# Weight sums of a block product made by accumulating DMAs from GpSimd in place of VectorE additions

## Chip, cores and metric

The kernel runs on one core of a Trainium2 chip. The metric is the device time of one execution in microseconds (us). The engines are named as in the profile: PE (TensorE matmuls), PEld (its weight loads), DVE (VectorE), ACT (ScalarE), POOL (GpSimd) and SP (SyncE, which issues most DMAs). SPq and POOLq are the DMA queues of SP and POOL.

## The reference, cut to what matters

The model is a two-layer decoder trunk on 256 tokens of width 2048 in float32. Layer 0 is an 8-head retention mixer, layer 1 a pooling mixer. The change touches heads 1 to 7 of layer 0 alone.

```python
def retention_branch(xn, w_in, w_out):              # 8 heads, dk 256, dv 512, chunk 128
    q, k, v, g = jnp.split(xn @ w_in, ...)          # w_in: 2048 x 12288
    q = rotate_pairs(q, cos, sin)
    k = rotate_pairs(k, cos, sin) * (dk ** -0.5)
    # scores = (q k^T) * decay, y = scores v (and the state between chunks)
    y = (y - mean(y)) * rsqrt(var(y) + GN_EPS)      # per head
    return (jax.nn.silu(g) * y) @ w_out
```

## The kernel before

Every float32 product is made of three float32r matmuls: both operands are split into a high part (hi) and a rest (lo), and hi*hi, hi*lo and lo*hi are summed in PSUM. The activations are split once (`xa_hi`, `xa_lo`). The weights stream through in units of 128 x 1024 floats (512 KB). For each unit SP loads the raw weights into one of eight slots (`w_raw`), ACT copies them to `w_hi` (`head_hi`, L841 to L850), DVE subtracts to get `w_lo` (`head_lo`, L1228 to L1233), and PE multiplies. `w_hi` and `w_lo` are rings of four units, so ACT can start a unit only when PE has used the unit four places before it (semaphore `unit_used`). `hi_ready` and `lo_ready` count the finished splits.

Heads 1 to 7 are one loop, and each of its passes works through 40 units in the order of the table `ORDER` (L80). Units h0 to h3 and A2 to A7 give q and k, C4 to C7 the right half of v, B4 to B7 the right half of the gate g, and O0 to O7 the output projection of the head before. The left half of v and g is not multiplied out directly. It is made with a Strassen-like scheme of seven block products M1 to M7 (each in two units, a and b). Their weights are blocks X1 to X4 of the raw stream or sums of them: M1, M2 and M3 use X1, X4 and X3 as loaded. M5 uses X1+X2, M6 uses X1+X2+X3, M4 uses X1+X2+X3+X4, and M7 uses X2+X3. A unit of M takes 6 matmuls of 512 columns on PE, a unit of A, B, C or O 12.

Before the change, DVE makes these sums: eight additions a head (`t1_sum`, `t2_sum`, `t3_sum`, `t4_sum`, all recorded at L1237) into two buffers `t1_raw` and `t3_raw`, counted by `t_ready`. ACT and DVE then split a sum as they split any unit. The function `head` of each engine says after which unit (`u`) its other steps stand: on DVE the gating of the head before (`gate_y`), the rotation of q and k (`rotate`), the corrections of the accumulators from PSUM snapshots (`fix_c`, `fix_b`); on ACT the copies around two DMA transposes a head (`y_halves`, `y_words`, `qk_halves`, `qk_words`). SP issues the loads in the order of `HEAD_LOADS` (name, slot, the last unit that reads the slot), and the two transposes at `Y_TURN` and `QK_TURN` in the same queue. In the first head, DVE makes four sums of activations (`form_sums`, `f_raw`, L1266), all after unit 19.

Of the kernel before, what the change touches and what calls it, by code (L numbers as in the profile page):

```python
# [80 lines left out]
         "C4 M6a C5 M6b C6 M7a C7 M7b O0 M4a O1 M4b B4 M2a M2b O2 O3 O4 O5 O6 O7 B5 B6 B7").split()  # L81
# [4 lines left out]
HEAD_LOADS = (("A0", 3, "h1"), ("A1", 0, "h3"), ("A2", 1, "A2"), ("X1a", 2, "M1b"), ("X2a", 3, "M3b"), ("A3", 4, "A3"), ("X1b", 5, "M3a"),  # L86
# [7 lines left out]
SUM_OF = {"M5": 0, "M6": 4, "M7": 2, "M4": 6}  # L94
SUMS = 2 * FORMS
# [36 lines left out]
def trunk(nc, stream, first0, first1, second, third, fourth, x, xT, pT, gains, pool_scale, final_gain, rope, decay, wider, counts, ident, out):  # L132
    with ExitStack() as ctx:
# [69 lines left out]
        t1_raw = at("t1_raw", 32, [P, UNIT, UNIT * COL], F32)  # L203
        t3_raw = at("t3_raw", 24, [P, UNIT, UNIT * COL], F32)
# [91 lines left out]
        t_ready = sem("t_ready")  # L296
# [169 lines left out]
        def _(pool):  # L466
            pool.wait_ge(xT_landed[NC - 1], 16)
# [6 lines left out]
            pool.dma_start(p_raw, pT).then_inc(p_landed, 16)  # L474

# [9 lines left out]
        def _(pe):  # L485
# [149 lines left out]
            def head(hd, base):  # L635
# [41 lines left out]
                product_part("M2a", base, acc["B"][0][:], *a12, False)  # L677
                product_part("M2b", base, acc["B"][0][:], *a12, False)
# [13 lines left out]
                g_unit(5, base)  # L692
# [136 lines left out]
        def _(act):  # L829
# [11 lines left out]
            def head_hi(hd, u, base):  # L841
# [5 lines left out]
                if name[:2] in SUM_OF:  # L847
                    act.wait_ge(t_ready, hd * SUMS + (SUM_OF[name[:2]] + "ab".index(name[2]) + 1 - SUMS))
# [224 lines left out]
            def head(hd, base):  # L1073
                for u in range(HEAD_S):
                    head_hi(hd, u, base)
                    if u == 3:
                        g_sigmoid(hd - 1, base)
                    if u == 6:
# [3 lines left out]
                    if u == 14:  # L1082
                        y_words(hd - 1)
                    if u == 21:
# [3 lines left out]
                    if u == 25:  # L1088
# [3 lines left out]
                    if u == 30:  # L1092
                        act.wait_ge(lo_ready, base + (AT["M4b"] + 1))
# [131 lines left out]
        def _(dve):  # L1225
# [9 lines left out]
            def quad_sum(hd, dst, in0, in1):  # L1235

                dve.tensor_tensor(dst, in0, in1, ALU.add).then_inc(t_ready, 1)  # L1237

            def t1_sum(hd, i):
                ab = "ab"[i]  # L1240
                wait_head_landed(dve, hd, "X1" + ab)
                wait_head_landed(dve, hd, "X2" + ab)
                quad_sum(hd, t1_raw[:, i, :], slot(SLOT["X1" + ab]), slot(SLOT["X2" + ab]))

            def t3_sum(hd, i):
                ab = "ab"[i]
                wait_head_landed(dve, hd, "X3" + ab)
                quad_sum(hd, t3_raw[:, i, :], slot(SLOT["X2" + ab]), slot(SLOT["X3" + ab]))

            def t2_sum(hd, i, base):  # L1250
                dve.wait_ge(lo_ready, base + (AT[("M5a", "M5b")[i]] + 1))
                quad_sum(hd, t1_raw[:, i, :], t1_raw[:, i, :], slot(SLOT[("X3a", "X3b")[i]]))

            def t4_sum(hd, i, base):
                dve.wait_ge(lo_ready, base + (AT[("M6a", "M6b")[i]] + 1))
                wait_head_landed(dve, hd, ("X4a", "X4b")[i])
                quad_sum(hd, t1_raw[:, i, :], t1_raw[:, i, :], slot(SLOT[("X4a", "X4b")[i]]))

            def form_sums():
# [24 lines left out]
            def fix_c(hd, base):  # L1284
# [4 lines left out]
                own.mark(dve.tensor_tensor(fix_v[:], snap_u3[:], side[1][:], ALU.subtract))  # L1289
                own.wait()  # L1290
# [82 lines left out]
            def rotate(hd, done, a_reads):  # L1373

                dve.wait_ge(unit_used, done)
                for t in range(TT):
# [145 lines left out]
            def first_head():  # L1522
                first_units_lo()
                for u in range(2, 3 * KD_U):
# [13 lines left out]
                    if u == 19:  # L1538
                        form_sums()
# [11 lines left out]
            def head(hd, base):  # L1551
                for u in range(HEAD_S):
                    head_lo(u, base)
                    if u == 4:
                        gate_y(hd - 1)
                    if u in (6, 8):
                        t1_sum(hd, (u - 6) // 2)
                    if u in (10, 12):
                        t3_sum(hd, (u - 10) // 2)
                    if u in (14, 16):  # L1560
                        t2_sum(hd, (u - 14) // 2, base)
                    if u in (22, 24):
                        t4_sum(hd, (u - 22) // 2, base)
                    if u == 20:
                        y_lo_part(hd - 1, False)
                    if u == 18:
                        rotate(hd, base + (AT["A7"] + 1), hd * 3 - 1)
                    if u == 26:
                        qkT_lo_part(hd, False)
                    if u == 28:  # L1570
                        fix_c(hd, base)
                    if u == 31:
# [320 lines left out]
```

## Time and profile before

| | |
|---|---|
| median of 3 runs | 1557.14 us (1557.06 to 1558.04) |
| the profiled execution | 1558.86 us, of which 1557.0 us span |
| PE busy | 1533.6 us (98% of the span), clock 0.997 of full |
| DVE, ACT busy | 1154.0 us (74%), 928.4 us (60%) |
| POOL busy | 4.6 us |
| HBM read | 297.40 MB, 192 GB/s over the span |

The span runs from the first to the last instruction, and the execution's own time has 1.86 us around it. "Busy" is the time in which an engine had an instruction in work. For PE it is a modelled time of overlapping matmuls, so that the starts of matmuls tell stalls better than the busy share does. The first head takes the first 84.6 us, heads 1 to 7 some 89.8 us each up to 712.9 us, and the rest follows.

### The profile page before, as it was taken

Reading aid. Unit: us, or ns where it says so; the run is one execution under the profiler, and the core shown is the slowest. Engines: PE = TensorE matmul, PEld = TensorE weight load, DVE = VectorE, ACT = ScalarE, POOL = GpSimd, SP = SyncE. Lnnn points to the kernel's source line nnn. Section 1 sums busy time; section 2 is a strip of 40 time slices with the busy share of each in tenths; the row PEclk is TensorE's granted clock in tenths of the full one; section 3 lists DMA queues with packets and bytes.
Section 4 is the critical chain, followed back from the end, with each engine's and each line's share of the span. In section 5 each row is a group of like instructions: output and inputs, shape, how many; then the busy total and the mean of one; then the engine's idle time right before and its main releaser. Section 6 shows DMA issues by size and latency. Waiting matters only on the chain.

```text
span 1557.0 us, 19965 instructions
## 1 busy us (share of the span) xinstructions
PE 1533.6 (98%) x6788; PEld 1258.6 (81%) x6788; DVE 1154.0 (74%) x1418; ACT 928.4 (60%) x1108; POOL 4.6 (0%) x12
## 2 busy tenths in 40 slices
PE   9999999999999999999999999999999999999997
PEld 7777878878787888878888888888888888888885
DVE  6889888888989888897756585775577557755665
ACT  7466574746657474755767556644664466446843
POOL 0000000000000000000000000000000000000000
PEclk9999999999999999999999999999999999999999
DMA  9475565747666575775566666755765576555651
GB/s 382 161 244 181 192 207 189 216 152 252 197 191 196 186 200 177 230 226 176 189 230 205 202 220 196 244 190 190 217 216 209 192 214 217 216 202 190 218 194 76
DMA packets 133497, 318.42 MB, mean 205 GB/s; under 512 B 80544, under 2 KB 80560, under 8 KB 112336
## 3 DMA queue, kind: packets, MB, share of 16 engines
q1 hardware_dynamic: 132608, 314.35, 61.2%
q0 software_dynamic: 704, 3.27, 0.6%
q8 instruction: 25, 0.41, 0.1%
q10 hardware_dynamic: 144, 0.26, 0.0%
q14 instruction: 16, 0.13, 0.0%
HBM read 297.40 MB, written 2.10 MB: 192 GB/s over the span
## 4 chain that ended last, share of the span: by engine, by line
PE 77%; DVE 10%; issue 5%; ACT 4%; DMA 3%; SPq 1%; DVEq 0%; ACTq 0%
PE accA L493 10%; PE accA L495 10%; PE accA L494 10%; PE accC L493 9%; PE accC L494 9%; PE accC L495 9%; PE accB L493 5%; PE accB L495 5%; PE accB L494 5%; DVE w_lo L1232 4%; DMA halvesT_e<-halves_e 2%; ACT words_e L929 2%; ACT w_hi L850 1%; PE accA L513 1%; PE accA L511 1%
## 5 line engine op out<-in xcount | busy, mean ns | idle before, releaser
L1304 DVE TENSOR_TENSOR w_lo<-w_raw,w_hi 128x1024 fp32r<-128x1024 f32 x326 | 395.4, 1222 | 227.9 <-ACT w_hi L839 226.0
L839 ACT CAST w_hi<-w_raw 128x1024 fp32r<-128x1024 f32 x326 | 340.0, 1052 | 267.8 <-PE accA L495 100.5
L850 ACT CAST w_hi<-w_raw 128x1024 fp32r<-128x1024 f32 (+1 forms) x224 | 220.2, 998 | 193.1 <-PE accC L495 68.1
L1232 DVE TENSOR_TENSOR w_lo<-w_raw,w_hi 128x1024 fp32r<-128x1024 f32 (+1 forms) x224 | 254.7, 1151 | 62.5 <-ACT w_hi L850 62.0
L493 PE MATMUL accA<-w_hi,xa_hi 128*128 128x512 f32 x452 | 176.1, 390 | 1.4 <-DVE w_lo L1232 0.9
L495 PE MATMUL accA<-w_hi,xa_lo 128*128 128x512 f32 x452 | 175.9, 389 | 0.0
L494 PE MATMUL accA<-w_lo,xa_hi 128*128 128x512 f32 x452 | 175.8, 389 | 0.0
L493 PE MATMUL accC<-w_hi,xa_hi 128*128 128x512 f32 x396 | 154.2, 389 | 0.0
L494 PE MATMUL accC<-w_lo,xa_hi 128*128 128x512 f32 x396 | 154.1, 389 | 0.0
L495 PE MATMUL accC<-w_hi,xa_lo 128*128 128x512 f32 x396 | 154.1, 389 | 0.0
L493 PEld LDWEIGHTS accA<-w_hi,xa_hi 128*128 128x128 f32 x452 | 84.8, 188 | 19.8 <-DVE w_lo L1232 1.3
L495 PEld LDWEIGHTS accA<-w_hi,xa_lo 128*128 128x128 f32 x452 | 84.8, 188 | 17.8
L494 PEld LDWEIGHTS accA<-w_lo,xa_hi 128*128 128x128 f32 x452 | 84.8, 188 | 17.5
L495 PEld LDWEIGHTS accC<-w_hi,xa_lo 128*128 128x128 f32 x396 | 74.3, 188 | 15.5
L493 PEld LDWEIGHTS accC<-w_hi,xa_hi 128*128 128x128 f32 x396 | 74.3, 188 | 15.4
L494 PEld LDWEIGHTS accC<-w_lo,xa_hi 128*128 128x128 f32 x396 | 74.3, 188 | 15.4
L1232 DVE TENSOR_TENSOR w_lo<-t_raw,w_hi 128x1024 fp32r<-128x1024 f32 x56 | 68.2, 1218 | 11.8 <-ACT w_hi L850 11.8
L493 PE MATMUL accA<-w_hi,oT_hi 128*128 128x512 f32 x184 | 72.4, 393 | 0.1
L493 PE MATMUL accC<-w_hi,oT_hi 128*128 128x512 f32 x184 | 72.1, 392 | 0.0
L494 PE MATMUL accA<-w_lo,oT_hi 128*128 128x512 f32 x184 | 71.7, 390 | 0.0
L495 PE MATMUL accA<-w_hi,oT_lo 128*128 128x512 f32 x184 | 71.6, 389 | 0.0
L494 PE MATMUL accC<-w_lo,oT_hi 128*128 128x512 f32 x184 | 71.6, 389 | 0.0
(277 smaller groups left out, 2951.6 us busy)
## 6 DMA issues: line engine op xcount, KB each, us to landing
w_raw<-in_stream_dram SPq DMA_DIRECT2D x162, 1024.0 KB, 4.8
w_raw<-in_stream_dram SPq DMA_DIRECT2D x224, 512.0 KB, 5.0
h<-in_x_dram SPq DMA_DIRECT2D x4, 512.0 KB, 13.3
xT_raw<-in_xT_dram SPq DMA_DIRECT2D x3, 512.0 KB, 14.6
dec<-in_decay_dram POOLq DMA_DIRECT2D x1, 1024.0 KB, 9.0
fgain<-in_final_gain_dram POOLq DMA_DIRECT2D x1, 1024.0 KB, 7.3
out_dram<-emb SPq DMA_DIRECT2D x1, 1024.0 KB, 3.8
halvesT_e<-halves_e SPq DMA_TRANSPOSE x56, 6.0
```

What stands on the lines that cost most here:

```text
L493: pe.matmul(acc[pair][t][:, 0:n], xh, wh, start=first and b == 0, stop=False, skip_group_check=onto)
L494: pe.matmul(acc[pair][t][:, 0:n], xh, wl, start=False, stop=False, skip_group_check=onto)
L495: mm = pe.matmul(acc[pair][t][:, 0:n], xl, wh, start=False, stop=last and b == UNIT - 1, skip_group_check=onto)
L511: pe.matmul(acc[pair][t][:], xh, w_hi[:, u % RING, 0:COL], start=first, stop=False)
L513: mm = pe.matmul(acc[pair][t][:], xl, w_hi[:, u % RING, 0:COL], start=False, stop=False)
L839: act.copy(w_hi[:, r % RING, :], w_raw[:, r // 2, (r % 2) * 1024:(r % 2 + 1) * 1024]).then_inc(hi_ready, 1)
L850: act.copy(dst, unit_raw(name)).then_inc(hi_ready, 1)
L929: act.copy(dst[:].bitcast(U16).rearrange("p k (n two) -> p two k n", two=2)[:, i, :, :], bufs[1][:, 4 * i:4 * i + 4, :]).then_inc(words_re ...
L1232: dve.tensor_tensor(w_lo[:, u % RING, 0:n], unit_raw(ORDER[u]), w_hi[:, u % RING, 0:n].bitcast(F32), ALU.subtract).then_inc(lo_ready, 1)
L1304: dve.tensor_tensor(w_lo[:, r % RING, :], w_raw[:, r // 2, (r % 2) * 1024:(r % 2 + 1) * 1024], w_hi[:, r % RING, :].bitcast(F32), ALU.subt ...
```

## The change

The eight sums of a head are no longer made on DVE. GpSimd issues eight DMAs (`add_block`) that read the block to be added again from HBM and add it onto the slot in which the first block lies (`accum_op=ALU.add`). X1's two slots become X1+X2, then X1+X2+X3, then X1+X2+X3+X4, and X2's two slots become X2+X3. GpSimd waits for the `w_lo` of the unit that last reads the old content and, for the second and third sum of X1, for the sum before. ACT waits for the landing of the sum (`sum_landed`) in place of `t_ready`. The 32 plain loads of a head stay, with other slots and another order. Steps are moved as well: gating two units later, the rotation in two halves and one step earlier, `y_words` five units later, `qk_words` and the halves two or three later, the unit B5 between M2a and M2b, and `form_sums` in four pieces after units 13, 15, 17 and 19.

```diff
 ORDER = ("h0 h1 h2 h3 A2 M1a A3 M1b A4 M3a A5 M3b A6 M5a A7 M5b "
-         "C4 M6a C5 M6b C6 M7a C7 M7b O0 M4a O1 M4b B4 M2a M2b O2 O3 O4 O5 O6 O7 B5 B6 B7").split()
+         "C4 M6a C5 M6b C6 M7a C7 M7b O0 M4a O1 M4b B4 M2a B5 M2b O2 O3 O4 O5 O6 O7 B6 B7").split()
...
-Y_TURN, QK_TURN = "C4", "O2"
+Y_TURN, QK_TURN = "C5", "B4"
...
+            def add_block(hd, base, x, term, used):
+
+                n = names.index(term + x[2])
+                at = hd * (HEAD_U // (2 * RAW)) + ((RET1 - HEAD_U + n) // (2 * RAW))
+                pool.wait_ge(lo_ready, base + (AT[used] + 1))
+                pool.dma_start(slot(SLOT[x]), rounds[at, n // 2 % RAW, :, n % 2 * UNIT * COL:(n % 2 + 1) * UNIT * COL],
+                               accum_op=ALU.add).then_inc(sum_landed[x], 16)
+
+            def head_sums(hd, base):
+
+                add_block(hd, base, "X1a", "X2", "M1a")
+                add_block(hd, base, "X1b", "X2", "M1b")
+                wait_head_landed(pool, hd, "X2a")
+                add_block(hd, base, "X2a", "X3", "M1b")
+                wait_head_landed(pool, hd, "X2b")
+                add_block(hd, base, "X2b", "X3", "M1b")
+                pool.wait_ge(sum_landed["X1a"], hd * 48 - 32)
+                add_block(hd, base, "X1a", "X3", "M5a")
+                pool.wait_ge(sum_landed["X1b"], hd * 48 - 32)
+                add_block(hd, base, "X1b", "X3", "M5b")
+                pool.wait_ge(sum_landed["X1a"], hd * 48 - 16)
+                add_block(hd, base, "X1a", "X4", "M6a")
+                pool.wait_ge(sum_landed["X1b"], hd * 48 - 16)
+                add_block(hd, base, "X1b", "X4", "M6b")
...
                 if name[:2] in SUM_OF:
-                    act.wait_ge(t_ready, hd * SUMS + (SUM_OF[name[:2]] + "ab".index(name[2]) + 1 - SUMS))
+                    x, n = SUM_OF[name[:2]]
+                    each = 48 if x == "X1" else 16
+                    act.wait_ge(sum_landed[x + name[2]], hd * each + (n * 16 + 16 - each))
...
-                    if u == 14:
+                    if u == 19:
                         y_words(hd - 1)
...
-                    if u == 19:
-                        form_sums()
+                    if u in (13, 15, 17, 19):
+                        form_sums((u - 13) // 2)
...
-                    if u in (6, 8):
-                        t1_sum(hd, (u - 6) // 2)
-                    if u in (10, 12):
-                        t3_sum(hd, (u - 10) // 2)
-                    if u in (14, 16):
-                        t2_sum(hd, (u - 14) // 2, base)
-                    if u in (22, 24):
-                        t4_sum(hd, (u - 22) // 2, base)
...
-                    if u == 18:
-                        rotate(hd, base + (AT["A7"] + 1), hd * 3 - 1)
+                    if u in (17, 19):
+                        rotate(hd, base + (AT["A7"] + 1), hd * 3 - 1, ((u - 17) // 2,))
+                    if u == 20:
+                        rotated(hd * 3 - 1)
```

On POOL, between the loads of the first head and those of layer 1, the queue before holds five DMAs with nothing between `p` (into `sig`) and `wide`:

```order
L473 DMA dec<-in_decay_dram 128x2048 [waits rope_landed]
L474 DMA sig<-in_pT_dram 128x1024
L477 DMA wide<-in_wider_dram 128x12 [waits yT_done]
L478 DMA inv<-in_counts_dram 128x1024
L481 DMA fgain<-in_final_gain_dram 128x2048 [waits d_ready]
```

After the change the sums of each head stand between them. These are the first six of a head, which are X1a, X1b, X2a, X2b, X1a again and X1b again:

```order
L495 DMA sig<-in_pT_dram 128x1024
L468 DMA w_raw<-in_stream_dram 128x1024 [waits lo_ready] x2
L468 DMA w_raw<-in_stream_dram 128x1024 [waits lo_ready,head_landed3]
L468 DMA w_raw<-in_stream_dram 128x1024 [waits lo_ready,head_landed6]
L468 DMA w_raw<-in_stream_dram 128x1024 [waits lo_ready,sum_landed_X1a]
L468 DMA w_raw<-in_stream_dram 128x1024 [waits lo_ready,sum_landed_X1b]
```

Eight such DMAs a head (56 in all) now stand in one queue, each behind the ones before it; the last two wait as the two before them do.

On ACT, before the change, these rows follow the split of M5a: A7, then `y_words` (words and oT), then M5b, which reads `t_raw`:

```order
L850 CAST w_hi<-w_raw 128x1024 [waits head_landed7,unit_used]
L927 ISA [waits qkT_ready]
L929 COPY words_e<-halvesT_e 128x1024 [waits halvesT_landed]
L929 COPY words_e<-halvesT_e 128x1024
L964 ISA
L966 CAST oT_hi<-words_e 128x512 [waits words_ready]
L966 CAST oT_hi<-words_e 128x512
L844 REGISTER_ALU
L848 REGISTER_ALU [waits unit_used]
L850 CAST w_hi<-t_raw 128x1024 [waits t_ready]
L844 REGISTER_ALU
L850 CAST w_hi<-w_raw 128x1024 [waits head_landed5,unit_used]
```

After the change, from the split of M6a on, `y_words` stands behind the split of M6b, which waits for the second sum of X1b, and ahead of that of C6:

```order
L876 CAST w_hi<-w_raw 128x1024 [waits sum_landed_X1a]
L868 REGISTER_ALU
L358 REGISTER_ALU [waits unit_used]
L876 CAST w_hi<-w_raw 128x1024 [waits head_landed0]
L876 CAST w_hi<-w_raw 128x1024 [waits sum_landed_X1b,unit_used]
L953 ISA [waits qkT_ready]
L955 COPY words_e<-halvesT_e 128x1024 [waits halvesT_landed]
L955 COPY words_e<-halvesT_e 128x1024
L989 ISA
L991 CAST oT_hi<-words_e 128x512 [waits words_ready]
L991 CAST oT_hi<-words_e 128x512
```

So what delays M6b's sum delays `y_words` and C6 as well.

On DVE, before the change, the rows from the split of M6a to that of M6b have the whole rotation in one piece:

```order
L1232 TENSOR_TENSOR w_lo<-t_raw,w_hi 128x1024
L1230 REGISTER_ALU
L1232 TENSOR_TENSOR w_lo<-w_raw,w_hi 128x1024
L1378 SCALAR_TENSOR_TENSOR qk<-accA,rs,ropec 128x512
L1383 SCALAR_TENSOR_TENSOR qk_56<-accA,rs,ropes 128x512
L1378 SCALAR_TENSOR_TENSOR qk<-accA,rs,ropec 128x512
L1383 SCALAR_TENSOR_TENSOR qk_56<-accA,rs,ropes 128x512
L1390 ISA
L1391 TENSOR_TENSOR qk<-qk,qk_56 128x1024
L1230 REGISTER_ALU
L1232 TENSOR_TENSOR w_lo<-t_raw,w_hi 128x1024
```

After the change the sums are gone and a unit's split stands between the halves of the rotation:

```order
L1256 TENSOR_TENSOR w_lo<-w_raw,w_hi 128x1024
L1385 SCALAR_TENSOR_TENSOR qk<-accA,rs,ropec 128x512
L1390 SCALAR_TENSOR_TENSOR qk_56<-accA,rs,ropes 128x512
L1254 REGISTER_ALU
L1256 TENSOR_TENSOR w_lo<-w_raw,w_hi 128x1024
L1254 REGISTER_ALU
L1256 TENSOR_TENSOR w_lo<-w_raw,w_hi 128x1024
L1385 SCALAR_TENSOR_TENSOR qk<-accA,rs,ropec 128x512
L1390 SCALAR_TENSOR_TENSOR qk_56<-accA,rs,ropes 128x512
L1254 REGISTER_ALU
L1256 TENSOR_TENSOR w_lo<-w_raw,w_hi 128x1024
```

The addition of the two rotated parts (L1391 before) has moved one unit further.

## Rows read from the trace of the kernel before

**Rows 1.** Busy time by stretch (a head; the rest of the kernel).

```profile
core 0: us, PE busy (x) PEld busy (x) DVE busy (x) ACT busy (x) POOL busy (x), PEclk, DMA share, GB/s
...
264.10:353.90 89.80, 88.84 (x395) 72.44 (x394) 77.69 (x98) 54.28 (x61) 0.00 (x0) 1.00 0.64 198
...
712.80:1557.00 844.20, 833.30 (x3708) 689.92 (x3706) 545.16 (x625) 501.43 (x616) 1.59 (x3) 1.00 0.60 200
```

**Rows 2.** PE in order of time, head 3: start us, duration us.

```profile
298.91 0.39 PE L495 MATMUL accC<-w_hi,xa_lo 128*128 128x512 f32 x1
299.56 0.50 PE L525 MATMUL side<-w_hi,f_hi 128*128 128x512 f32 x1 [0.27 <-DVE w_lo L1232]
...
301.06 0.39 PE L493 MATMUL accC<-w_hi,xa_hi 128*128 128x512 f32 x1
...
321.79 0.40 PE L527 MATMUL accB<-w_hi,xa_lo 128*128 128x512 f32 x1
322.85 0.49 PE L525 MATMUL accB<-w_hi,xa_hi 128*128 128x512 f32 x1 [0.67 <-DVE w_lo L1232]
```

**Rows 3.** Who waited for whom, engine PE: us in total, times, longest.

```profile
PE accB L525 <- DVE w_lo L1232: 4.7, 7, 0.7
...
PE side L525 <- DVE w_lo L1232: 1.8, 7, 0.3
```

**Rows 4.** Busy time by stretch, end of the first head (columns: rows 1).

```profile
63.00:84.00 21.00, 18.70 (x73) 14.29 (x72) 16.65 (x35) 9.97 (x15) 0.00 (x0) 0.92 0.06 16
```

**Rows 5.** The order of time on PE, end of the first head.

```profile
66.82 0.39 PE L495 MATMUL accB<-w_hi,xa_lo 128*128 128x512 f32 x1
69.04 0.50 PE L594 MATMUL side<-v_hi,pr_hi 128*128 128x512 f32 x1 [1.83 <-DVE pr_lo L1400]
```

**Rows 6.** Instruction groups on DVE, first head: busy us, mean ns.

```profile
L1266 DVE TENSOR_TENSOR f_raw<-f_raw,xa_lo 128x512 f32<-128x512 f32 x6 | 4.2, 693 | 0.2
```

**Rows 7.** Groups of instructions on DVE, head 3.

```profile
L1237 DVE TENSOR_TENSOR t_raw<-t_raw,w_raw 128x1024 f32<-128x1024 f32 x4 | 4.9, 1216 | 0.0
L1237 DVE TENSOR_TENSOR t_raw<-w_raw 128x1024 f32<-128x1024 f32 x4 | 4.9, 1216 | 0.0
```

**Rows 8.** The order of time on DVE, head 3.

```profile
283.58 1.22 DVE L1232 TENSOR_TENSOR w_lo<-t_raw,w_hi 128x1024 fp32r<-128x1024 f32 x1
...
297.15 1.22 DVE L1391 TENSOR_TENSOR qk<-qk,qk 128x1024 f32<-128x1024 f32 x1
298.29 1.22 DVE L1232 TENSOR_TENSOR w_lo<-t_raw,w_hi 128x1024 fp32r<-128x1024 f32 x1
```

**Rows 9.** DMA issues by line: KB each, median us from issue to landing.

```profile
w_raw<-in_stream_dram SPq DMA_DIRECT2D x224, 512.0 KB, 5.0
...
fgain<-in_final_gain_dram POOLq DMA_DIRECT2D x1, 1024.0 KB, 7.3
...
inv<-in_counts_dram POOLq DMA_DIRECT2D x1, 512.0 KB, 5.3
```

**Rows 10.** Busy time by stretch within that head (columns: rows 1).

```profile
264.00:276.00 12.00, 12.00 (x54) 9.87 (x53) 10.51 (x11) 9.32 (x10) 0.00 (x0) 1.00 0.71 255
276.00:282.00 6.00, 6.00 (x28) 4.97 (x27) 5.31 (x6) 2.83 (x4) 0.00 (x0) 1.00 0.93 186
282.00:294.00 12.00, 12.00 (x55) 9.93 (x54) 10.36 (x10) 10.33 (x11) 0.00 (x0) 1.00 0.85 276
294.00:301.00 7.00, 6.73 (x30) 5.27 (x29) 6.97 (x9) 4.69 (x5) 0.00 (x0) 1.00 0.49 162
```

**Rows 11.** The order of time on PE, head 3, last matmul of M3b.

```profile
283.95 0.39 PE L527 MATMUL accC<-w_hi,f_lo 128*128 128x512 f32 x1
```

**Rows 12.** The order of time on ACT, head 3.

```profile
283.98 2.58 ACT L929 COPY words_e<-halvesT_e 128x1024 uint16<-128x1024 uint16 x2
286.58 1.14 ACT L966 CAST oT_hi<-words_e 128x512 fp32r<-128x512 f32 x2
287.63 1.05 ACT L850 CAST w_hi<-t_raw 128x1024 fp32r<-128x1024 f32 x1
```

More of the change, by code:

```diff
@@ L85 @@
 MORE = (HEADS - 1) * (HEAD_S - HEAD_U)
-HEAD_LOADS = (("A0", 3, "h1"), ("A1", 0, "h3"), ("A2", 1, "A2"), ("X1a", 2, "M1b"), ("X2a", 3, "M3b"), ("A3", 4, "A3"), ("X1b", 5, "M3a"),
[4 rows of a table removed]
+HEAD_LOADS = (("A0", 3, "h1"), ("A1", 0, "h3"), ("A2", 2, "A2"), ("X1a", 1, "M4a"), ("A3", 3, "A3"), ("X1b", 4, "M4b"), ("A4", 5, "A4"),
[4 rows of a table added]
 SLOT = {name: slot for name, slot, _last in HEAD_LOADS}
 LOADS_OF = {b: [name for name, slot, _last in HEAD_LOADS if slot == b] for b in range(2 * RAW)}
-Y_TURN, QK_TURN = "C4", "O2"
-SUM_OF = {"M5": 0, "M6": 4, "M7": 2, "M4": 6}
-SUMS = 2 * FORMS
+Y_TURN, QK_TURN = "C5", "B4"
+SUM_OF = {"M5": ("X1", 0), "M6": ("X1", 1), "M4": ("X1", 2), "M7": ("X2", 0)}
 O_RET = -NC
@@ L295, in trunk @@
         c_read = sem("c_read")
-        t_ready = sem("t_ready")
+        sum_landed = {x: sem(f"sum_landed_{x}") for x in ("X1a", "X1b", "X2a", "X2b")}
         snap_ready = sem("snap_ready")
@@ L474, in _ @@
             pool.dma_start(p_raw, pT).then_inc(p_landed, 16)
+            for hd in range(1, HEADS):
+                head_sums(hd, hd * HEAD_S + (RET1 - HEAD_S))
             pool.wait_ge(yT_done, 1)
@@ L1091, in head @@
                         snapshot(snap_u3, base + (AT["M7b"] + 1))
-                    if u == 30:
-                        act.wait_ge(lo_ready, base + (AT["M4b"] + 1))
+                    if u == 29:
                         act.wait_ge(c_fixed, hd * 2)
@@ L1233, in head_lo, with form_sums @@
                                   ).then_inc(lo_ready, 1)
[L1235 to L1259, printed above, removed]
+            def form_sums(i):
                 def a(t, half, src):
@@ L1282, in forms_lo, with fix_w @@
                     dve.tensor_tensor(f_lo[i][:], f_raw[i][:], f_hi[i][:].bitcast(F32), ALU.subtract).then_inc(f_ready, 1)
-            def fix_c(hd, base):
+            def fix_w(hd, base):
                 dve.wait_ge(unit_used, base + (AT["C7"] + 1))
@@ L1289, in fix_c @@
                 own.mark(dve.tensor_tensor(fix_v[:], snap_u3[:], side[1][:], ALU.subtract))
+            def fix_c():
                 own.wait()
@@ L1371, in first_units_lo, with rotate @@
                                           ).then_inc((first_lo, lo_ready)[b], 1)
-            def rotate(hd, done, a_reads):
+            def rotate(hd, done, a_reads, tiles=range(TT)):
                 dve.wait_ge(unit_used, done)
-                for t in range(TT):
+                for t in tiles:
                     heads = acc["A"][t][:].rearrange("p (two d) -> p two d", d=DK)
@@ L1388, in rotate, with rotated @@
                         op0=ALU.mult, op1=ALU.mult)
+                if TT - 1 not in tiles:
+                    return
                 ins.then_inc(a_read, 1)
+                if len(tiles) == TT:
+                    rotated(a_reads)
+            def rotated(a_reads):
                 dve.wait_ge(a_read, a_reads)
```

48 lines of the change are left out of this document (25 added, 23 removed), and 8 rows, old and new, of the table HEAD_LOADS.

## The prediction

> **What bounds the kernel now.** I read the busy times by stretch first [rows 1]. A pass of the head loop takes 89.8 us, PE is busy in 88.84 of them and its clock is granted in full; after the loop it is 833.3 of 844.2. So PE sets the pace and all that a change in the loop can give is PE's small stalls. The order of time on PE shows two of them [rows 2]. A matmul starts 0.23 us after the one before where nothing is missing (six of them, from 299.56 to 301.06, take 1.5 us with the first dearer). M6b's first starts 0.65 after its predecessor and takes 0.50 in place of 0.39: 0.42 + 0.11 = 0.53 lost. M2b's first starts 1.06 after: 0.83 + 0.10 = 0.93 lost. The waits say that both are waits for DVE's `w_lo`, and that they come in each of the seven heads [rows 3]. With M2a, which waits for the same but shorter, I count 1.8 us a head.
>
> Why DVE is late for M6b is seen in its order of time [rows 8]: the rotation's last addition starts at 297.15 and M6b's split only at 298.29, behind it. The eight sums cost DVE 4.9 + 4.9 = 9.8 us a head [rows 7], while DVE is busy 77.69 of 89.8 [rows 1].
>
> The first head has one large stall: PE starts nothing between 66.82 and 69.04, while it waits for `pr_lo` on DVE [rows 5], and the clock granted over the 21 us around it is 0.92 [rows 4].
>
> **The change part by part.**
>
> *DVE's sums go, the rotation is split, B5 stands ahead of M2b.* DVE loses 9.8 us a head. M6b's split no longer has five rotation steps before it, and M2b gets a unit of 12 matmuls (2.7 us) as cover. The whole gain is at most the 1.8 us. DVE still makes `fix_c`, `v_lo` and `qkT_lo` within the units from M4b to M2b, so that a part of M2a's and B5's stall may stay. Bounds 0.9 and 1.8; I take 1.2 us a head.
>
> *`form_sums` in four pieces.* Ten additions of 0.69 us six of them shown in [rows 6] stood in one block of some 7 us ahead of the work that `pr_lo` needs; now each piece of 1.4 to 2.1 us stands behind another unit. The stall is worth 2.22 - 0.23 + 0.11 = 2.1 us [rows 5], and the lower clock 0.08 x 21 = 1.7 us [rows 4]. If PE does not stop, I expect that the clock stays. Bounds 2.1 and 3.8; I take 3.8, once.
>
> *Eight accumulating DMAs a head.* No row shows one. The nearest is a plain copy of 512 KB issued by GpSimd, 5.3 us from issue to landing; one of 1024 KB took 7.3 [rows 9]. What the DMA engines need for 512 KB (0.524 MB) comes from the stretch in which they move most: 0.85 of their time for 276 GB/s [rows 10], so 0.524 / 276 x 0.85 = 1.6 us of all engines. An accumulation must read two operands, the block in HBM and the slot in SBUF. I therefore price it at twice the copy, 3.2 us of the engines, and at 5.3 + 1.6 = 6.9 us from issue to landing where nothing else is under way. Bounds: 1.6 and 5.3 (as a copy); 4.8 and 8.5 (three passes).
>
> The Trainium skill, "Collectives: The Full Stack", section "The bandwidth ceiling: the fold count and why AG ≠ RS ≠ AR", says that an addition in the DMA's datapath is slow for its two source reads, and gives 62.28 against 32.35 GB/s, a ratio of 1.93. An estimate by that page is 1.6 x 1.93 = 3.1 us for a piece and a total of some 1577 us by the sum below; no run here shows it yet.
>
> *What waits for them.* The tightest is the second sum of X1b, for M6b. It can be issued when M5b is split. M5b can be split when PE has used M3b, whose last matmul ends at 283.95 + 0.39 = 284.3 [rows 11]; with 1.05 on ACT [rows 12] and 1.22 on DVE [rows 8] that is 286.6. It must have landed when ACT has to begin M6b's copy. C6's first matmul would stand at 301.06 - 0.53 = 300.5 without the stall [rows 2]. Ahead of it are its `w_lo` (1.2), its copy (1.05), then, now behind M6b, `y_words` with 2.58 + 1.14 = 3.7 [rows 12], and M6b's own copy (1.05): 300.5 - 7.0 = 293.5. So there are 293.5 - 286.6 = 6.9 us. That is what a lone accumulation takes, with nothing to spare. Behind ACT's wait stand `y_words`, C6 and every later copy, then DVE's splits, then PE.
>
> But it is not alone. From 264 to 294 us, the stretch up to this point, the engines are used 0.71 x 12 + 0.93 x 6 + 0.85 x 12 = 24.3 of 30 us [rows 10], which leaves 5.7. Into it fall five accumulations (both first sums of X1, both of X2, the second of X1a), and the second of X1b behind them. Five at 3.2 are 16.0 us, 10.3 more than is free. Two loads of the stretch (C7 and O0) may land later at no cost, 2 x 1.6 = 3.2; and the stretch from 276 to 282, with the transposes, is used 0.93 for only 186 GB/s, which by the rate of the next one needs 186 / 276 x 0.85 = 0.57, so up to 0.36 x 6 = 2.1 us of it may be waiting and not work. That leaves 10.3 - 3.2 - 2.1 = 5.0 us by which M6b's sum is late. Bounds: 0 (as copies: 8.0 - 5.7 - 3.2 < 0) and 10.3 (no load slips). I take 5.0, nearer the two-read price than the copy. The other sums have eight units or more before they are needed, some 16 us.
>
> *The moved loads and turns* issue the same 32 loads and four transposes from SP; their 5.0 us to landing [rows 9] is covered by four to six units (8 to 12 us). I cost them at nothing beyond the crowding above.
>
> **Sum.** 7 x (5.0 - 1.2) - 3.8 = +22.8 us on the profiled execution's 1558.9, which is 1581.7. That execution is 1.7 us above the median of the runs, so I forecast **1580 us**, slower.
>
> **Rivals.**
>
> *Faster: the sums land in time.* If an accumulation costs the engines what a copy does, the backlog is below nothing, it lands in 5.3 of the 6.9 us, and what is left is the gain: 7 x 1.2 + 3.8 = 12 us, 1545; at the bounds 7 x 1.8 + 3.8 = 16, 1541, and 7 x 0.9 + 2.1 = 8, 1549. For it: half of the engines' time after 294 is free (0.49 used [rows 10]). Against it: the two reads. It decides below about 2.2 us of engines a piece (5 x 2.2 = 11 = 5.7 + 3.2 + 2.1). The skill's "SBUF — State Buffer", section "The DMA setup-cost knee (why "@ 1 MiB" ≠ asymptote)", gives a GpSimd DMA 2 us and its bytes at 436 GB/s, thus 3.2 us for 512 KB; the trace has 5.3 [rows 9], so by the trace this page speaks less for this rival than it seems.
>
> *Nothing measurable.* A delay of 1.2 + 3.8 / 7 = 1.7 us a head eats the whole gain: 1557. It needs a price between the two, near 2.5 us.
>
> *The DMA engines become the bound of the whole head.* They are used 0.64 of 89.8 = 57.5 us [rows 1], so 32.3 are free, and eight accumulations reach that at 4.0 us each. At three passes (4.8) they are 6.1 over, 7 x 6.1 - 3.8 = +39, 1596; at four (6.4), 7 x 18.9 - 3.8 = +128, 1685.
>
> **How the numbers follow.** The forecast (late by 2 to 7 us a head) has 0.48, the engines as bound 0.10, the copy's price 0.30, nothing measurable 0.12. Measured runs spread by 0.06%, and I take 0.2% (3.1 us) as what can be told from no change. That gives slower 0.58, same 0.12, faster 0.30. The range goes from the fast rival's best, 1541, to 10.3 late in each head without a slip, 7 x (10.3 - 1.2) - 3.8 = +60, 1616; four passes lie outside. The forecast's own range is 1560 to 1600 (2 to 7 us late: +2 to +37).
>
> **What would show it.** Right: in the trace after, ACT's copy of M6b (or M6a) waits for the accumulating DMA in every head, PE stalls at M6a, C5 or C6 by 2 to 7 us a head, the pass of a head is above 92 us, the GpSimd issues land 8 us or more after issue, and the DMA share from M1a to M6b is at 0.95 or more. The first head's stall before its values is gone and its clock is full; `t_raw` is gone from DVE. Wrong: the accumulations land within 7 us, no copy waits for them, and a pass is under 89 us.

## The result and the profile after

The changed kernel takes 1602.78 us (median of 4 runs, 1600.77 to 1606.72) against 1557.10 for the kernel before (4 runs): 1.0298 times as long, 95% interval 1.0284 to 1.0311. It is slower, as forecast, but by 45.7 us and not by 22.8.

The passes of the head loop, by stretch (columns as in [rows 1]):

```profile
core 0: us, PE busy (x) PEld busy (x) DVE busy (x) ACT busy (x) POOL busy (x), PEclk, DMA share, GB/s
79.10:182.70 103.60, 91.37 (x393) 74.71 (x394) 70.42 (x93) 53.56 (x60) 6.91 (x8) 0.93 0.79 214
182.70:277.10 94.40, 91.39 (x395) 74.67 (x394) 69.33 (x90) 53.86 (x60) 6.92 (x8) 0.96 0.78 233
277.10:371.10 94.00, 88.95 (x395) 72.57 (x394) 69.35 (x90) 53.81 (x60) 6.92 (x8) 1.00 0.78 234
371.10:464.30 93.20, 90.00 (x395) 73.51 (x394) 69.26 (x90) 53.78 (x60) 6.92 (x8) 0.98 0.78 236
464.30:558.00 93.70, 90.22 (x395) 73.79 (x394) 69.34 (x90) 53.79 (x60) 6.92 (x8) 0.98 0.78 235
558.00:660.50 102.50, 91.17 (x395) 74.88 (x394) 69.25 (x90) 53.78 (x60) 6.92 (x8) 0.93 0.82 215
660.50:754.60 94.10, 89.47 (x391) 72.81 (x390) 69.06 (x89) 55.19 (x60) 6.95 (x8) 0.98 0.84 250
```

A pass had 89.8 us [rows 1]. Five passes now have 93.2 to 94.4, two have 103.6 and 102.5. DVE is freer, as it had to be (69.3 busy for 77.7). PE's busy time grew too: where the clock is below 1.00, matmuls ran at half speed for a while.

What PE and ACT waited for, in all (us, times, longest), and how the accumulations stand among the DMA issues and queues of the page:

```profile
PE side L549 <- DVE w_lo L1256: 35.5, 7, 11.8
PE accC L517 <- DVE w_lo L1256: 6.3, 7, 1.6
...
ACT w_hi L876 <- DMA w_raw<-in_stream_dram: 100.6, 27, 16.5
...
q0 software_dynamic: 8768, 32.63, 10.9%
...
w_raw<-in_stream_dram POOLq DMA_DIRECT2D x56, 512.0 KB, 8.7
```

One stall in each of the seven heads, 35.5 us together, behind a copy of ACT that waits for a DMA. The page before has `q0 software_dynamic: 704, 3.27, 0.6%`, so the 56 accumulations took (0.109 x 1601.1 - 0.006 x 1557.0) / 56 = 2.95 us of all 16 engines each.

The place, in the second pass, from the orders of time on DVE, POOL, ACT and PE:

```profile
201.91 1.23 DVE L1256 TENSOR_TENSOR w_lo<-w_raw,w_hi 128x1024 fp32r<-128x1024 f32 x1 [0.21 <-ACT w_hi L876]
...
205.34 1.75 POOL L468 DMA_DIRECT2D w_raw<-in_stream_dram  x2 [6.15 <-DMA w_raw<-in_stream_dram]
...
215.74 1.99 ACT L876 CAST w_hi<-w_raw 128x1024 fp32r<-128x1024 f32 x2 [6.91 <-DMA w_raw<-in_stream_dram]
...
215.28 0.39 PE L519 MATMUL accC<-w_hi,xa_lo 128*128 128x512 f32 x1
218.10 0.50 PE L549 MATMUL side<-w_hi,f_hi 128*128 128x512 f32 x1 [2.43 <-DVE w_lo L1256]
...
220.55 0.80 PE L517 MATMUL accC<-w_hi,xa_hi 128*128 128x512 f32 x1 [0.58 <-DVE w_lo L1256]
221.14 0.63 PE L518 MATMUL accC<-w_lo,xa_hi 128*128 128x512 f32 x1
221.57 0.63 PE L519 MATMUL accC<-w_hi,xa_lo 128*128 128x512 f32 x1
```

The first row is M5a's split, done at 203.1; from then on X1a's second sum could be issued. But POOL works in order and stands 6.15 us at the sum ahead of it, which waits for the load of X2b. X1a's sum is the second of the two issues in the row at 205.34, some 2.8 us late (205.9), and it lands 9.8 us later, when ACT's copy of M6a starts (215.74). PE stalls at M6a by 2.6 us. Behind the stall matmuls take 0.63 us for 0.39 and start 0.43 us apart for 0.23: the granted clock is 0.50 from 219.4 to 226.0, the lower of its two levels (1.2 of 2.4 GHz).

### The profile page after: what moved, and what is told of

It is laid out like the page before. It is cut to its first block, busy times and chain, and to the rows that moved or that the text cites. A ratio compares the mean times of both kernels' runs of the same rounds, so it can differ in the third digit from the quotient of the medians.

```text
span 1601.1 us, 19968 instructions
## 1 busy us (share of the span) xinstructions
PE 1542.9 (96%) x6788; PEld 1267.9 (79%) x6788; DVE 1095.2 (68%) x1362; ACT 924.5 (58%) x1108; POOL 53.1 (3%) x68
## 3 DMA queue, kind: packets, MB, share of 16 engines
q0 software_dynamic: 8768, 32.63, 10.9%
## 4 chain that ended last, share of the span: by engine, by line
PE 78%; DMA 8%; issue 5%; ACT 4%; DVE 4%; POOL 1%; SPq 0%; ACTq 0%; DVEq 0%; POOLq 0%
PE accC L517 9%; PE accC L518 9%; PE accC L519 9%; PE accA L517 9%; PE accA L519 9%; PE accA L518 9%; DMA w_raw<-in_stream_dram 8%; PE accB L517 5%; PE accB L519 5%; PE accB L518 5%; ACT w_hi L876 1%; DVE w_lo L1256 1%; ACT words_e L955 1%; POOL w_raw L468 1%; PE side L549 1%
## 5 line engine op out<-in xcount | busy, mean ns | idle before, releaser
L1256 DVE TENSOR_TENSOR w_lo<-w_raw,w_hi 128x1024 fp32r<-128x1024 f32 (+1 forms) x280 | 320.9, 1167 | 173.4 <-ACT w_hi L876 172.3
L876 ACT CAST w_hi<-w_raw 128x1024 fp32r<-128x1024 f32 (+1 forms) x280 | 275.2, 1007 | 268.8 <-DMA w_raw<-in_stream_dram 100.6
L517 PE MATMUL accC<-w_hi,xa_hi 128*128 128x512 f32 x396 | 159.1, 402 | 6.3 <-DVE w_lo L1256 6.3
L519 PEld LDWEIGHTS accA<-w_hi,xa_lo 128*128 128x128 f32 x452 | 84.9, 188 | 17.6
L519 PE MATMUL accC<-w_hi,oT_lo 128*128 128x512 f32 x184 | 71.7, 390 | 0.0
```

The source lines that it names most:

```text
L517: pe.matmul(acc[pair][t][:, 0:n], xh, wh, start=first and b == 0, stop=False, skip_group_check=onto)
L519: mm = pe.matmul(acc[pair][t][:, 0:n], xl, wh, start=False, stop=last and b == UNIT - 1, skip_group_check=onto)
L876: act.copy(dst, unit_raw(name)).then_inc(hi_ready, 1)
L1256: dve.tensor_tensor(w_lo[:, u % RING, 0:n], unit_raw(ORDER[u]), w_hi[:, u % RING, 0:n].bitcast(F32), ALU.subtract).then_inc(lo_ready, 1)
```

## Experiments

Theories, named alike in the expectations: A, the accumulations crowd the DMA engines; B, the order of POOL's queue issues X1's second sums late; C, the DMA engines stand still (their packets are open, but few bytes move) while y's transposes and accumulations overlap. All diffs but those said otherwise are against the changed kernel.

**The sums taken out (no_sums).**

```diff
-            for hd in range(1, HEADS):
-                head_sums(hd, hd * HEAD_S + (RET1 - HEAD_S))
...
-                    act.wait_ge(sum_landed[x + name[2]], hd * each + (n * 16 + 16 - each))
```

> The changed kernel without any of the 56 accumulations and without the waits for them (M5, M6 and M4 use X1 as it is, M7 uses X2, so the output isn't the reference's). It is what is left of the change when the sums cost nothing. Theory A (the moves are worth what I named, the sums' transfers cost all of the loss): 1541 to 1547. Rival (the moves themselves lose: new load order, B5, y's words later): 1552 or more, with stalls at the same units in every head.

Measured: 1542.09 us, ratio 0.9900 (0.9884 to 0.9917). Two passes by stretch:

```profile
166.90:254.70 87.80, 87.80 (x395) 72.89 (x394) 69.26 (x90) 54.12 (x60) 0.00 (x0) 1.00 0.62 203
254.70:342.40 87.70, 87.70 (x395) 72.85 (x394) 69.24 (x90) 54.12 (x60) 0.00 (x0) 1.00 0.63 203
```

PE never stops. So the moves gain 15.5 us (2.0 a pass and 1.5 once), and the accumulations, with all that waits for them, cost 1602.8 - 1542.1 = 60.7, which is 8.7 a head. The rival, that the moves themselves lose, is out.

**Plain copies in their place (plain_copies).**

```diff
-                               accum_op=ALU.add).then_inc(sum_landed[x], 16)
+                               ).then_inc(sum_landed[x], 16)
```

> The eight GpSimd DMAs of a head stay where they are, with their waits, but copy the block over the slot and add nothing (M5, M6, M4 and M7 then use other weights than the reference). Theory A (the price of the second operand: a packet of 4 KB took 0.33 us in the accumulation and 0.16 to 0.17 in a plain load): the eight cost 8 x 1.3 = 10.5 us less of all DMA engines in a head, M6a's block lands in 6 to 7 us in place of 9.4 to 20, no stall is over 1 us, and the time is 1545 to 1555. Theory B (the order of GpSimd's queue: X1a's second sum is issued only when the load of X2b has landed, 2.6 us late in head 2): the stall at M6a goes down by the shorter landing alone and 0.5 to 1.5 us of it stay, 1555 to 1565. Theory C (the transposes and any GpSimd transfer stand still beside each other): two passes of some 102 us stay, 1575 to 1590.

Measured: 1559.93 us, 1.0010 (0.9999 to 1.0021), which is in B's range and above A's. Its page, the fourth pass, and four stretches in it:

```profile
q0 software_dynamic: 8768, 32.63, 6.2%
...
w_raw<-in_stream_dram POOLq DMA_DIRECT2D x56, 512.0 KB, 6.5
...
352.60:447.60 95.00, 90.80 (x395) 74.69 (x394) 69.24 (x90) 53.79 (x60) 4.22 (x8) 0.96 0.74 232
...
372.00:376.00 4.00, 4.00 (x19) 3.30 (x19) 2.44 (x3) 2.11 (x2) 1.04 (x2) 1.00 0.98 251
376.00:380.00 4.00, 4.00 (x20) 3.30 (x19) 2.28 (x2) 1.05 (x1) 0.53 (x1) 1.00 1.45 111
380.00:384.00 4.00, 4.00 (x19) 3.34 (x18) 0.00 (x0) 0.00 (x0) 0.00 (x0) 1.00 0.96 122
384.00:388.00 4.00, 1.59 (x8) 0.97 (x6) 0.00 (x0) 0.57 (x1) 0.00 (x0) 1.00 1.00 393
```

A copy takes (0.062 x 1562.3 - 9.3) / 56 = 1.56 us of the engines, an accumulation 1.89 times that. In this order of the queues the addition is thus 42.9 of the 60.7 us, and 17.8 are left at a copy's price. That is no share of A alone: the runs below take most of the 60.7 away with all additions in place. And two passes (93.8 and 95.0 us) have a stall of 4 us at M6a with copies too. In the second of them the engines moved 111 and 122 GB/s while their packets were open all the time: the standstill needs no addition.

**X1's second sums first in POOL's queue (x1_first).**

```diff
                 add_block(hd, base, "X1b", "X2", "M1b")
+                pool.wait_ge(sum_landed["X1a"], hd * 48 - 32)
+                add_block(hd, base, "X1a", "X3", "M5a")
+                pool.wait_ge(sum_landed["X1b"], hd * 48 - 32)
+                add_block(hd, base, "X1b", "X3", "M5b")
                 wait_head_landed(pool, hd, "X2a")
...
-                add_block(hd, base, "X1b", "X3", "M5b")
```

> Only the order of GpSimd's queue is changed: the second sums of X1a and X1b, for M6, are issued ahead of the two sums of X2, for M7, so that they don't wait for the loads of X2. Theory B (queue order): X1a's second sum is issued when M5a is split, 2.6 us earlier in head 2, the stall of 2.3 to 2.6 us at M6a in five passes goes, and with it the half clock behind it, 3 to 5 us a pass; 1575 to 1585. Theory A (the DMA engines are too busy): the landing grows by what the issue gains, M6a stays late by 1.5 us or more, and M7a may be late in its place; 1592 to 1602. Theory C (the y transposes stand beside the accumulations): the two long passes of 102 to 104 us stay or move to other heads.

Measured: 1578.32 us, 1.0135 (1.0118 to 1.0152), in B's range, and no pass is over 94 us. The first and the sixth pass, then ACT and PE in the second:

```profile
78.80:172.70 93.90, 89.96 (x393) 73.93 (x394) 70.66 (x93) 53.73 (x60) 6.94 (x8) 0.98 0.80 236
...
542.70:634.40 91.70, 88.35 (x395) 72.74 (x394) 69.26 (x90) 53.78 (x60) 6.96 (x8) 1.00 0.80 240
...
207.41 1.05 ACT L876 CAST w_hi<-w_raw 128x1024 fp32r<-128x1024 f32 x1 [4.58 <-DMA w_raw<-in_stream_dram]
208.36 2.57 ACT L955 COPY words_e<-halvesT_e 128x1024 uint16<-128x1024 uint16 x2
210.96 1.14 ACT L991 CAST oT_hi<-words_e 128x512 fp32r<-128x512 f32 x2
212.01 2.94 ACT L876 CAST w_hi<-w_raw 128x1024 fp32r<-128x1024 f32 x3
...
211.03 0.39 PE L551 MATMUL side<-w_hi,f_lo 128*128 128x512 f32 x1
214.36 0.55 PE L517 MATMUL accC<-w_hi,xa_hi 128*128 128x512 f32 x1 [2.94 <-DVE w_lo L1256]
214.71 0.63 PE L518 MATMUL accC<-w_lo,xa_hi 128*128 128x512 f32 x1
```

This is the stall of the prediction: M6b's copy waits for X1b's second sum, `y_words` (3.7 us) stands behind it, and C6 has it as 3.1 us on PE (214.36 - 211.03 - 0.23), with the half clock behind it. The new order is worth 24.5 us, but not for B's reason alone. B expected 3 to 5 us in each of the five shorter passes. In the profiled execution 26.7 us go, and 20.5 of them are the two long passes (103.6 to 93.9 and 102.5 to 91.7), which C had said would stay or move. The second to fifth give 0.6 to 2.2 us each, because the stall went from M6a to C6. That the time came out in B's range is luck. The standstill is gone too, though the transposes still overlap with the sums (in the first pass they are issued from 94.96 to 103.3, the sums at 101.7 and 104.9): in steps of 4 us, none in the loop has a DMA share of 0.8 or more and less than 140 GB/s.

**y's transposes as plain DMAs (y_no_transpose).**

```diff
-                        transpose_halves(in_emb, halvesT_landed)
+                        for t in range(TT):
+                            sp.dma_start(in_emb[1][:].rearrange("p (i k) n -> p i k n", i=2)[:, :, 2 * t:2 * t + 2, :],
+                                         in_emb[0][:, t, :, :].rearrange("p i (k n) -> p i k n", n=SEQ)
+                                         ).then_inc(halvesT_landed, 16)
```

> The two transposing DMAs of y in each head are replaced by two plain DMAs of the same bytes in packets of 1 KB (y goes into the output projection untransposed, so the output isn't the reference's). All accumulations stay. Theory C (the standstill of the DMA engines while transposes and accumulations overlap): the passes of 102 to 104 us are gone, the stalls at M6a fall to 0 to 0.5 us, and the time is 1550 to 1560. Theory A (engines busy with accumulations): only the engines' time of the transposes is saved, some 2 us a head, the stalls at M6a stay at 1 to 2 us, 1570 to 1585. Theory B (queue order): as now but for the two long passes, some 1582.

Measured: 1598.05 us, 1.0261 (1.0244 to 1.0279): none of the three ranges. SP's queue in the second pass, first of the changed kernel, then of this one:

```profile
198.72 8.88 SPq L407 DMA_TRANSPOSE halvesT_e<-halves_e  x2
207.85 2.73 SPq L425 DMA_DIRECT2D w_raw<-in_stream_dram  x4
```

```profile
192.81 1.32 SPq L418 DMA_DIRECT2D halvesT_e<-halves_e  x2
194.39 10.05 SPq L428 DMA_DIRECT2D w_raw<-in_stream_dram  x4
...
176.80:271.90 95.10, 91.12 (x395) 74.66 (x394) 69.35 (x90) 53.77 (x60) 6.92 (x8) 0.96 0.76 232
...
198.00:204.00 6.00, 6.00 (x28) 4.95 (x28) 3.67 (x3) 2.72 (x3) 2.61 (x3) 1.00 1.05 318
204.00:210.00 6.00, 5.76 (x26) 4.44 (x24) 0.00 (x0) 0.00 (x0) 0.00 (x0) 1.00 1.05 274
```

The transposes kept SP's own queue for 8.9 us. Without them the loads from C5 on go out 17.6 us into the pass (194.4 - 176.8) and not 25.2 (207.9 - 182.7), ahead of X1a's second sum, and every pass has a stall at M6a: the first takes 98.5 us, the others some 95. A standstill like that of the changed kernel (4 us with a share above 1.00 at less than 140 GB/s) is nowhere in its loop. But the edit also moved the loads, and x1_first has no standstill with all its transposes. So C is wrong as the main cause, and that the transposes make the standstill is not shown.

**Two steps on ACT and SP, from x1_first on.** First y's words behind C6's copy (x1_first_y20):

```diff
-                    if u == 19:
+                    if u == 20:
                         y_words(hd - 1)
```

> The kernel with X1's second sums first in GpSimd's queue, and y's words one unit later on ScalarE, behind C6's copy and not ahead of it. There every pass had one stall of 3.1 us at C6, since C6's copy stood behind the late copy of M6b and 3.7 us of y's words. If it is that order, the stall falls below 1 us and the half clock behind it goes too: 7 x (2.5 to 4.5) less, 1546 to 1562. Rival: the 3.7 us only move on, M7a or O0 stalls by 2 us or more, 1568 to 1578.

Measured: 1568.46 us, 1.0068 (1.0051 to 1.0084), at the lower end of the rival's range. C6's stall is 0.8 us at most, as forecast, and no other reaches the rival's 2 us; smaller ones, up to 1.6 us, stand at several units. Then, on top of it, two entries of SP's queue (x1_hold_c7; the first line is cut out of a longer one): C7's load waits until C5 is split, and B4's load goes ahead of the transposes of q and k.

```diff
-              ... ("A7", 5, "A7"), ...
+              ... ("A7", 5, "C5"), ...
-Y_TURN, QK_TURN = "C5", "B4"
+Y_TURN, QK_TURN = "C5", "X4a"
```

> The kernel with X1's second sums first and y's words behind C6, with two more moves in SyncE's queue: C7's load waits until C5 is split (it was issued 6 us earlier and took the DMA engines ahead of X1b's second sum, which landed 9.5 us after issue), and B4's load stands ahead of the transposes of q and k (it was issued behind them and held ScalarE for 3.4 us). If both stalls that were left come from these two places in the queues, C6 loses below 0.5 us and the units from M2a to M2b below 0.6, 1.8 to 2.8 us a head less: 1548 to 1556, and with that at or below the kernel before. Rival (the engines' total is what counts; a load moved is a load late elsewhere): 1562 to 1568.

Measured: 1552.99 us, 0.9972 (0.9961 to 0.9982). This is the forecast range. With all eight accumulations, this version is 49.8 us below the changed kernel and 0.3% below the kernel before, and 10.9 of the 60.7 us are left. Its largest wait on PE, and its accumulations on the page:

```profile
PE side L549 <- ACT snap_u L880: 9.9, 7, 2.6
...
q0 software_dynamic: 8768, 32.63, 10.1%
```

An accumulation takes (0.101 x 1553.9 - 9.3) / 56 = 2.64 us of the engines here, 1.69 times a copy. The 2.95 of the changed kernel thus has waiting in it.

M7a waits until ACT has copied M6b's side sum, and this copy stands behind C7's, which stands behind `y_words`. Two tries to move `y_words` away, behind M7a's copy (x1_hold_y21, u 21 for 20) and behind M7a's copy and the snapshot (x1_hold_snap):

> The fastest kernel so far with y's words one unit further back on ScalarE, behind M7a's copy. There the stall left in a pass is 0.5 to 2.75 us at M7a, whose copy stands behind C6's late one and 3.7 us of y's words. If the order of these copies is what is left, M7a's stall falls below 0.5 us and the pass to some 88.3: 1545 to 1550. Rival: C7 or M7b, or O0 behind y's lower halves, takes the stall over, 1551 to 1556.

> The kernel with C7's load held, and on ScalarE the copy of the side sum of M6b (the snapshot that M7a has to wait for) ahead of y's words, both behind M7a's copy. With y's words behind M7a's copy alone, 4.2 us of PE's waits were still for that snapshot, 0.5 to 1.0 us a pass. If the sums' remaining cost is only these places in ScalarE's order, the passes come to 88 us, within 0.5 us of the passes without any sums (87.8), and the profiled execution to 1543 to 1548. If the accumulations cost by their transfers whatever the order, passes of 90 us or more remain in some heads, and the time is 1549 to 1555.

Measured: 1554.72 us, 0.9987 (0.9977 to 0.9996), and 1570.15, 1.0086 (1.0072 to 1.0100). The first is in its rival's range: the second to sixth profiled passes have 88.4 to 88.9 us and the span is 1548.7, but the runs reach from 1550.55 to 1559.20, so that nothing is won over x1_hold_c7. The second is above both of its ranges: the snapshot waits 2.0 us for PE, and C7 is late by 2.4 to 2.6 in every pass but the first. The last run's question is answered for neither side: order moved the stall, and did not remove it.

**The moves with the sums left on DVE.** All against the kernel before. dve_sums_moves takes B5 ahead of M2b, the split rotation and the feature sums in four pieces; b5_forms leaves the rotation whole; b5_turn also puts the transposes of q and k ahead of B5's load:

```diff
-         "C4 M6a C5 M6b C6 M7a C7 M7b O0 M4a O1 M4b B4 M2a M2b O2 O3 O4 O5 O6 O7 B5 B6 B7").split()
+         "C4 M6a C5 M6b C6 M7a C7 M7b O0 M4a O1 M4b B4 M2a B5 M2b O2 O3 O4 O5 O6 O7 B6 B7").split()
-Y_TURN, QK_TURN = "C4", "O2"
+Y_TURN, QK_TURN = "C4", "B5"
```

> The kernel before with its sums on VectorE, and only three of the other edits: B5 between M2a and M2b (with its load moved), the rotation split into two pieces and an addition, the feature sums of the first head in four pieces. If the gain that I named for these moves (1.2 us a head and up to 3.8 once) needs VectorE free of the sums, the time is 1552 to 1556 (only the first head's 2 to 4 us). If the moves are enough by themselves, 1541 to 1547. Rival: M6b and M2b stall elsewhere in the same head, 1556 or more.

> The kernel before, sums on VectorE and rotation in one piece, with only B5 ahead of M2b (and its load) and the feature sums of the first head in four pieces. The passes of 95 us with the rotation split (stalls of 2.1 us at M6b and at O0 in every head) should be gone if ScalarE's copy of the rotated q and k, which then came 4 us late, caused them: M2b's stall of 0.93 a head goes, 2.0 to 2.8 us go once, 1547 to 1551. Rival: the moved B5 or its load is the cause, 1580 or more.

> The kernel before, sums on VectorE, with B5 ahead of M2b, the feature sums in four pieces, and now the transposes of q and k issued ahead of B5's load (behind it they were issued when C7 had been split, and ScalarE waited 4.2 us for them in every head, which PE had as 3.5 us at O0). If that was the cause, the 3.5 us go: M2b's stall of 0.93 a head is gone too, 1547 to 1552. Rival: B5 ahead of M2b does not fit VectorE with its sums, 1557 or more.

Measured: 1597.29 us (1.0251, 1.0234 to 1.0269), 1584.52 (1.0170, 1.0153 to 1.0187) and 1556.04 (0.9990, 0.9981 to 0.9999). The first two came out as their rivals said, b5_turn between its two sides, 1 us below the rival's. The rows of PE's waits (dve_sums_moves), of ACT's (b5_forms, then b5_turn) and of PE's (b5_turn):

```profile
PE side L525 <- ACT snap_u L854: 13.5, 7, 1.9
```

```profile
ACT words_e L929 <- DMA halvesT_e<-halves_e: 30.5, 7, 5.0
```

```profile
ACT words_e L929 <- DMA halvesT_e<-halves_e: 5.3, 7, 1.0
...
PE accB L493 <- DVE w_lo L1232: 4.7, 7, 0.7
```

With the rotation split, PE has a stall of 13.5 / 7 = 1.9 us in each head, behind a copy of ACT, that b5_forms doesn't have. Behind B5's load in SP's queue the transposes of q and k kept ACT waiting for 30.5 / 7 = 4.4 us a head; ahead of it, for 0.8. But the stall that M2b had [rows 3] now stands at B5, with the same 4.7 us. In the kernel without the sums the same order of units has no stall. So B5's place gives nothing while DVE makes the sums.

**Only the sums with X4 as DMAs.** x4_dma on b5_forms, x4_dma_turn on b5_turn:

```diff
-                    if u in (22, 24):
-                        t4_sum(hd, (u - 22) // 2, base)
+                    pool.wait_ge(lo_ready, hd * HEAD_S + (RET1 - HEAD_S) + (AT[("M6a", "M6b")[i]] + 1))
+                    pool.dma_start(t1_raw[:, i, :], rounds[at_i, n // 2 % RAW, :, n % 2 * UNIT * COL:(n % 2 + 1) * UNIT * COL],
+                                   accum_op=ALU.add).then_inc(x4_added[i], 16)
```

> The same, and only the two sums with X4 (for M4) are made by accumulating DMAs of GpSimd, into the buffer of the sums; the other six stay on VectorE. They fall into the stretch after M6b, where the DMA engines have room, and had 5.4 to 6.0 us to landing in the changed kernel; M4a is needed some 8 units (20 us) after M6a's split. Theory A (cost is crowding): they land in 5 to 7 us, nothing waits for them, VectorE is 2.4 us a head freer, and the time is that of the one without them or up to 4 us less. Rival (any accumulation beside transposes or loads costs the pass): 4 us or more above it.

> The same, with the two sums with X4 made by accumulating DMAs of GpSimd. Theory A (an accumulation costs little where the DMA engines have room): as the one without them, or up to 4 us less, 1545 to 1552. Rival (an accumulation beside the transposes of q and k brings the standstill that the transposes of y had): 1560 or more, M4a late by 2 us or more.

Measured: 1595.83 us (1.0240, 1.0223 to 1.0257) and 1579.24 (1.0149, 1.0133 to 1.0164). For x4_dma_turn:

```profile
t_raw<-in_stream_dram POOLq DMA_DIRECT2D x14, 512.0 KB, 8.7
...
ACT words_e L942 <- DMA halvesT_e<-halves_e: 24.2, 7, 4.6
```

Nothing waits for the two sums. But the transposes of q and k, issued some microseconds behind them, now keep ACT for 24.2 us where they kept it for 5.3, and O0 is late in each head. The rival was right on the time, and wrong on the place: M4a is not late. Even in the stretch with room, two accumulations a head cost 3.3 us a head (1579.24 - 1556.04), through what waits beside them.

## Why the prediction came out as it did

**Right in the sum: the moves' gain.** 12 us forecast, 15.5 measured (no_sums). Both terms lie outside their bounds, and that they make up for each other is luck. The 1.2 us a head (at most 1.8) was 2.0, all of PE's stalls; the 3.8 once (at least 2.1) was too much: 1.5 us are left beside the passes, though the first head's stall is gone and its clock full, as the stretch of the changed kernel shows that answers to [rows 4]:

```profile
61.00:82.00 21.00, 20.43 (x89) 16.27 (x88) 17.80 (x38) 8.92 (x14) 0.00 (x0) 1.00 0.33 113
```

**Right: the price of a piece.** 1.6 us for a copy and 3.2 for an accumulation were 1.56 and 2.64 to 2.95. The Trainium skill's ratio of 1.93 ("Collectives: The Full Stack", "The bandwidth ceiling: the fold count and why AG ≠ RS ≠ AR") is that of two collectives; the measured 1.89 agrees with it in the changed kernel, the 1.69 of x1_hold_c7 is below it.

**Wrong in size: the term "5.0 us late a head".** It measured 8.7: five passes at 5.4 to 6.6 us above those of no_sums (87.8), two at 15.8 and 14.7. Three things were not in its working.

First, it took M6b's sum as the only tight one and let each sum be issued when its own operands were there. "The other sums have eight units or more before they are needed" is wrong for X1a's second sum: M6a stands four units behind M5a, as M6b behind M5b. POOL's queue is in order, so this sum also stood behind the wait for X2b's load, and M6a was the first to be late. Undoing the order alone gave back 24.5 us and left 36.2, which is 5.2 a head, with the stall where the prediction had it. That this is nearly its 5.0 is luck in part, for the stall is 3.1 us and the rest is not in its sum.

Second, the half clock behind a stall had no price. The seven passes have 61 matmuls of 0.63 us, which start 0.43 us apart in place of 0.23: some 12 us, 1.7 of the 8.7 a head. PE's whole busy time grew by more (90.4 us a pass in place of 87.8), also where the clock stayed full (88.95 in the third pass).

Third, the moved loads and turns were costed at nothing beyond the crowding, and the standstill stands where they meet the sums: some nine microseconds more in each of two passes. These are the same microseconds that x1_first gave back in its two passes, so the first and the third share don't add up. The share of the DMA engines, which the prediction took as work with 2.1 us of waiting in it, does not tell the two apart:

```profile
576.00:582.00 6.00, 6.00 (x28) 4.95 (x28) 4.24 (x4) 3.27 (x4) 1.75 (x2) 1.00 1.26 284
582.00:588.00 6.00, 6.00 (x28) 4.99 (x27) 1.65 (x2) 1.05 (x1) 0.86 (x1) 1.00 1.70 120
588.00:594.00 6.00, 2.96 (x14) 2.10 (x12) 0.00 (x0) 0.00 (x0) 0.00 (x0) 1.00 0.77 61
594.00:600.00 6.00, 0.00 (x0) 0.00 (x0) 0.00 (x0) 0.07 (x1) 0.00 (x0) 0.57 1.03 278
```

These are stretches of the sixth pass: the share is 1.70 and 0.77 while 120 and 61 GB/s move.

**The rivals.** That the sums cost a copy and all is hidden fell on both counts: the price is not a copy's, and at a copy's price the time is 1560, not 1545. The engines as the bound of the whole head would give a time like the measured one, but the share of a pass is 0.78 to 0.84 and a piece costs 2.95 at most, not 4.8. Of the signs that the prediction named, a copy of M6a or M6b waits in every head, the landing takes 8.7 us in the median, the share is 0.99 to 1.17 from 186 to 216 us, and the first head's clock is full; but PE's stalls are not all within 2 to 7 us, since two have over 11.

**Open.** Why the standstill comes in some passes and not in others, with the same order of issues, and why it is gone with x1_first, was not found; a kernel that keeps y's transposes apart from POOL's DMAs was not tried. How the 60.7 us divide between the additions and the order of the queues is not shown either: copies alone take 42.9 away, order alone 49.8. The best version stays 11 us above the kernel without sums.

## What to carry to other kernels

Price an accumulating DMA at nearly twice a copy of its bytes on all the engines (1.7 to 1.9 times here), and then look for what else in that stretch has a deadline: the loads, the transposes, the sums behind it in the same in-order queue. A sum that is needed early is issued ahead of sums that wait for loads, and loads that are needed late are held back until it has landed. When work leaves one engine, stalls elsewhere vanish only if the new path is in time: here the same eight DMAs gave 1602.8 or 1553.0 us by the order of three queues.

## What the runs showed of the hardware

With DMA transposes beside DMAs that GpSimd issues, the engines moved only 61 to 122 GB/s for 8 to 12 us in some passes, with additions or without (sixth pass of the changed kernel, fourth of plain_copies); beside SP's loads alone the transposes left 186 GB/s [rows 10]. It does not come each time: in x1_first they overlap as well, and no such stretch is there. The Trainium skill says in "DMA: Bandwidth & Descriptors", "Rules for kernel authors", that a transpose next to ordinary DMAs needs nothing. It says so of correctness, beside a warning of corrupted data, and these runs show a cost in time.

In the second, fourth and fifth pass of the changed kernel PE stood 2.3 to 2.6 us, and matmuls behind it took 0.63 us in place of 0.39. In the third pass it stood 2.4 us, and the granted clock is 1.00 over the whole pass.
